# Gated recurrent stage: the next head's value projection moves from the second-direction unit to the first-direction unit

## The chip, the core and the metric

The kernel runs on one core of one Trainium2 chip. The metric is the device time of one launch in microseconds, the median over repeated runs. The engines are TensorE (PE in the profile, PEld for its weight loads), VectorE (DVE), ScalarE (ACT), GpSimd (POOL) and SyncE (SP), which issues the transfers. Each works through its own list of instructions in order and waits on semaphores that the others raise.

## The reference, cut to what matters

The program computes two transformer-like blocks on 1024 tokens of width 1024. The change touches one part of the second block, a gated linear recurrence with 4 heads of 128 channels, run forward and backward over 256 context tokens and 1024 tokens:

```
v, k_f, k_b, lf_f, lf_b = hg_in            # projections of the modulated input
q = silu(split_heads(p[..., O_Q:O_G])) * HG_DK ** -0.5
o = hgrn2_bidir(q, v, k_f, k_b, lf_f, lf_b, s0_f, s0_b)
o = o * rsqrt(mean(o * o, -1) + EPS) * hg_norm_g
hg = o * silu(p[..., O_G:O_SC])
```

For each direction a chunk of 128 tokens is computed as scores (query times key times the decay between the two tokens) times values, plus query times a state carried from chunk to chunk. Each head needs five projections of width 128: the first direction's gate logits, the values, the queries, the second direction's gate logits, and the output gate. The values of a head serve both of its directions.

## The kernel before

The stage is `stage_hgrn`. It runs eight units, (head 0, direction 0), (head 0, direction 1), (head 1, direction 0) and so on. Units 0, 2, 4 and 6 are called even here (the first direction), the others odd. Nothing is planned at build time: the order on each engine is written out by hand, and the list `jobs` gives every PSUM user one of three pairs of banks in turn, so that a job waits until the job three before it has been read.

A unit on PE, in this order: transposes of the decayed keys (L2747, "kt"), the diagonal scores (L2751), seven levels of masked scores (`level(n, l)`, eight products of 128 columns at L2729, sixteen records each), the products of keys and values (L2761, "kv"), queries times states (L2776), and last scores times values (L2787). In between stand pieces of the next unit's projections (`front`, whose products are made at L198 in `split_matmuls`): Z0 and Z1 are the gate logits, V0 and V1 the values of chunks 0 to 7 and 8 to 9, QUERY and GATE the rest. The values have tokens as rows, so V0 is 192 products of 128 columns and V1 48 of them; QUERY and GATE are 48 of 512 columns, made in two halves. An even unit projects for the odd unit after it (Z0, Z1, GATE), an odd one for the next head's even unit (Z0, Z1, V0, V1, QUERY).

A level on DVE: `subtract` makes differences of cumulated decays (L2985 and L2986, or L2989 and L2990), ACT exponentiates (L2849), `weigh` multiplies in keys and queries (L2998, L2999), PE forms the scores, and `select` merges them under a mask (L3016). There are three buffers for a level's operand, so `subtract` of level l + 2 waits for PE to have finished level l - 1. DVE also does the next unit's preparation between levels: `softplus` (L2934 to L2936), `forget` (L2945 to L2953), `key_distance` (L2963) and `decayed_keys` (L2970). The next unit's kt waits for `decayed_keys`.

The weights come through a `WeightStream` of 20 tiles of 128 columns with one raw buffer and two split ones. ACT makes the upper half of a tile (`hi`, L233) and DVE the rest (`lo`, L237). In `front` on ACT the split of tile t + 2 is placed right behind the read of the last piece that used tile t:

```
if piece in LAST and tile + 2 < 5 * HG_HEADS:
    stream.hi(act, tile + 2)
```

On DVE `weights_lo(n, piece)` runs `stream.lo` of the same tile, which waits for that `hi`. It stands in the list of DVE at fixed levels of the unit: behind level 1 for Z1, level 3 for GATE, level 5 for V1 (ahead of `key_distance`), and at the end for QUERY.

Of the kernel before, what the change touches and what calls it, by code (L numbers as in the profile page):

```python
# [26 lines left out]
P = 128  # L27
# [30 lines left out]
HG_DK, HG_HEADS, HG_WIDTH = 128, 4, 512  # L58
# [2524 lines left out]
def stage_hgrn(k):  # L2583
# [13 lines left out]
    def take(*shape):  # L2597
# [4 lines left out]
    raw_at = at[0]; take(KD, P)  # L2602
    split_at = at[0]; take(2, KD, P)
# [13 lines left out]
    NL = len(LEVELS)  # L2617
    units = [(h, d) for h in range(HG_HEADS) for d in range(2)]
# [1 line left out]


    w_src = ins["w_in_2"].rearrange("o (k p) n -> p (o k) n", p=P)
    stream = WeightStream(k, [[w_src[:, :, s * HG_WIDTH + h * P:s * HG_WIDTH + (h + 1) * P]]
                              for h in range(HG_HEADS) for s in (1, 0, 3, 2, 4)], None, raw_at, split_at, n_raw=1)


    Z0, Z1, V0, V1, QUERY, GATE = "z0", "z1", "v0", "v1", "q", "g"
    PIECES = ({Z0: 0, Z1: 0, V0: 1, V1: 1, QUERY: 2}, {Z0: 3, Z1: 3, GATE: 4})
    LAST = (Z1, V1, QUERY, GATE)

    def has(n, piece):
        return n <= last_unit and piece in PIECES[units[n][1]]

    def tile_of(n, piece):
        return 5 * units[n][0] + PIECES[units[n][1]][piece]


    jobs = [(0, "front", piece) for piece in PIECES[0]]
    for n, (h, d) in enumerate(units):
        def front_of_next(*pieces):  # L2640
            return [(n + 1, "front", piece) for piece in pieces if has(n + 1, piece)]
        jobs += [(n, "kt", 0), (n, "kt", 1)] + front_of_next(Z0) + [(n, "level", NL), (n, "level", 0)] + \
                ([(n, "ss", 0)] if d == 0 and h else []) + [(n, "kv", 0), (n, "kv", 1)] + front_of_next(Z1) + \
                [(n, "level", 1)] + front_of_next(V0, GATE) + [(n, "level", 2), (n, "level", 3)] + front_of_next(V1) + \
                front_of_next(QUERY) + [(n, "level", l) for l in range(4, NL)]
    jobs.append((last_unit + 1, "ss", 0))

    def slot(job):
# [39 lines left out]
    with nc.Block() as block:  # L2688
# [5 lines left out]
        @block.tensor  # L2694
        def _(pe):
            def front(n, piece, steps=(0, 1)):

                if not has(n, piece):
                    return
                job, tile = (n, "front", piece), tile_of(n, piece)  # L2700
                if 0 in steps:
                    stream.ready(pe, tile)
                    wait_free(pe, job)
                if piece in (V0, V1):
                    chunks = range(8) if piece == V0 else range(8, NCH)
                    for i, c in enumerate(chunks):
                        if (2 * i) // len(chunks) in steps:
                            last = split_matmuls(pe, [banks(job)[:, i * P:(i + 1) * P]],
                                                 lambda s, kt: k.hT[:, s, kt, c * P:(c + 1) * P],
                                                 lambda s, kt, i: stream.part(tile, s, kt), KD)  # L2710
                else:
                    first, end = {Z0: (0, T), Z1: (T, TT)}.get(piece, (CTX, TT))
                    spans = [(a, min(a + HALF, end)) for i, a in enumerate(range(first, end, HALF)) if i in steps]
                    last = split_matmuls(pe, [banks(job)[:, a - first:e - first] for a, e in spans],
                                         lambda s, kt: stream.part(tile, s, kt),
                                         lambda s, kt, i: k.hT[:, s, kt, spans[i][0]:spans[i][1]], KD)
                if 1 in steps:
                    last.then_inc(made[slot(job)[0]], 1)

            def chunk_job(job, chunks, fn):  # L2720
                wait_free(pe, job)
                for i, c in enumerate(chunks):
                    last = fn(banks(job)[:, i * P:(i + 1) * P], c)
                last.then_inc(made[slot(job)[0]], 1)

            def level(n, l):
                pe.wait_ge(x_ready, NL * n + l + 1)
                v = x[:, buffer(n, l), :]
                chunk_job((n, "level", l), range(T // P), lambda out, c: pe.matmul(  # L2729
                    out, v[:, c * P:(c + 1) * P], v[:, c * P:(c + 1) * P], start=True, stop=True))  # L2730

            def sum_of_squares(n, h):
                pe.wait_ge(sq_done, h)
                job = (n, "ss", 0)
                wait_free(pe, job)
                for half in range(2):
                    last = pe.matmul(banks(job)[:, half * HALF:(half + 1) * HALF], k.ones[:, :],
                                     root[:, half * HALF:(half + 1) * HALF], start=True, stop=True)
                last.then_inc(made[slot(job)[0]], 1)

            for piece in PIECES[0]:
                front(0, piece)
            for n, (h, d) in enumerate(units):
                halves = (range(8), range(8, NCH))
                pe.wait_ge(kh_ready, n + 1)
                for i in range(2):
                    chunk_job((n, "kt", i), halves[i], lambda out, c: pe.transpose(out, kh[:, c, :], k.ident[:, :]))  # L2747
                front(n + 1, Z0, (0,))
                pe.wait_ge(k_ready, n + 1)
                pe.wait_ge(q_scaled, h + 1)  # L2750
                chunk_job((n, "level", NL), range(T // P), lambda out, c: pe.matmul(  # L2751
                    out, keys[:, n % 2, CTX + c * P:CTX + (c + 1) * P], q[:, h % 2, c * P:(c + 1) * P],
                    start=True, stop=True))
                level(n, 0)
                front(n + 1, Z0, (1,))
                if d == 0 and h:
                    sum_of_squares(n, h)
                pe.wait_ge(kt_done, 2 * n + 2)
                pe.wait_ge(v_done, 2 * h + 2)
                for i in range(2):  # L2760
                    chunk_job((n, "kv", i), halves[i], lambda out, c: pe.matmul(  # L2761
                        out, kh_t[:, c, :], vals[:, h % 2, c, :], start=True, stop=True))
                front(n + 1, Z1)
                level(n, 1)
                front(n + 1, V0, (0,))
                front(n + 1, GATE, (0,))
                level(n, 2)
                front(n + 1, V0, (1,))
                front(n + 1, GATE, (1,))
                level(n, 3)  # L2770
                pe.wait_ge(states_ready, n + 1)
                pe.wait_ge(qh_ready, n + 1)
                if d == 0 and h:
                    pe.wait_ge(o_free, h)
                for c in range(T // P):
                    last = pe.matmul(o_ps[:, c * P:(c + 1) * P], states[:, c, :], qh[:, c * P:(c + 1) * P],  # L2776
                                     start=d == 0 and c % 4 == 0, stop=False, skip_group_check=True)
                last.then_inc(inter_made, 1)
                front(n + 1, V1)
                front(n + 1, QUERY, (0,))  # L2780
                level(n, 4)
                front(n + 1, QUERY, (1,))
                for l in range(5, NL):
                    level(n, l)
                pe.wait_ge(selected, n + 1)
                for c in range(T // P):
                    last = pe.matmul(o_ps[:, c * P:(c + 1) * P], vals[:, h % 2, CCH + c, :], att[:, c * P:(c + 1) * P],  # L2787
                                     start=False, stop=d == 1, skip_group_check=True)
                last.then_inc(o_made, 1)
            sum_of_squares(last_unit + 1, HG_HEADS)  # L2790

        @block.scalar
        def _(act):
# [94 lines left out]
            for n, (h, d) in enumerate(units):  # L2888
# [11 lines left out]
                front(n + 1, Z1)  # L2900
                softplus_parts(n + 1)
                level(n, 4)
                front(n + 1, V0)
                front(n + 1, GATE)
                forget_parts(n + 1)
                level(n, 5)
                front(n + 1, V1)
                level(n, 6)
                front(n + 1, QUERY)
                decays(n + 1)  # L2910
            squares(HG_HEADS - 1)
            inverse_root(last_unit + 1)
# [2 lines left out]
        def _(dve):  # L2915
            link = chained(dve, v_ord)

            def weights_lo(n, piece):

                if has(n, piece) and tile_of(n, piece) + 2 < 5 * HG_HEADS:  # L2920
                    stream.lo(dve, tile_of(n, piece) + 2)
# [148 lines left out]
            for n, (h, d) in enumerate(units):  # L3070
# [3 lines left out]
                for l in range(1, NL):  # L3074
# [14 lines left out]
                    if l == 4:  # L3089
                        forget(n + 1)  # L3090
                    if l == 5:
                        weights_lo(n + 1, V1)
                        key_distance(n + 1)
                        subtract(n + 1, 0)
                subtract(n + 1, 1)
# [381 lines left out]
```

## Time and profile before

| what | value |
|---|---|
| median of 3 runs (lowest, highest) | 2919.38 us (2919.1, 2920.84) |
| the profiled execution's own time, its span | 2910.27 us, 2908.6 us |
| PE busy over the span | 2573.3 us (88%) |
| DVE busy, ACT busy | 1631.6 us (56%), 954.0 us (33%) |
| prologue of the stage with head 0's projections | about 1480 to 1537 us |
| unit 0, first kt to the next unit's kt | 1537.0 to 1603.1 us |
| unit 1 | 1603.1 to 1668.1 us |
| units 2 and 3 | to 1732.2 and 1798.8 us |
| units 4 and 5 | to 1865.6 and 1932.2 us |
| units 6 and 7 | to 1999.2 and about 2033 us |

The busy time of PE counts matmuls at whichever clock was granted, so a slow product adds to it. A unit's length is read from the start of its kt to the start of the next. A timeline row gives start, length, engine, line, operation, output and input, count, and in brackets the idle time ahead of it and the engine and line that ended it; rows that follow one another on one engine and line are merged, and the length is that of the merged row.

### The profile page before, as it was taken

Reading aid. Unit: us, or ns where it says so; the run is one execution under the profiler, and the core shown is the slowest. Engines: PE = TensorE matmul, PEld = TensorE weight load, DVE = VectorE, ACT = ScalarE, POOL = GpSimd, SP = SyncE. Lnnn points to the kernel's source line nnn. Section 1 sums busy time; section 2 is a strip of 40 time slices with the busy share of each in tenths; the row PEclk is TensorE's granted clock in tenths of the full one; section 3 lists DMA queues with packets and bytes.
Section 4 is the critical chain, followed back from the end, with each engine's and each line's share of the span. In section 5 each row is a group of like instructions: output and inputs, shape, how many; then the busy total and the mean of one; then the engine's idle time right before and its main releaser. Section 6 shows DMA issues by size and latency. Waiting matters only on the chain. (4 is left out here: it accounts for less than half of the span.)

```text
span 2908.6 us, 39503 instructions
## 1 busy us (share of the span) xinstructions
PE 2573.3 (88%) x16801; PEld 1379.2 (47%) x16801; DVE 1631.6 (56%) x2102; ACT 954.0 (33%) x1099; POOL 34.6 (1%) x61
## 2 busy tenths in 40 slices
PE   7977685999999999998866878796887999999997
PEld 4446462444444444444434757576332444444443
DVE  6667746654444443533226666667656676766243
ACT  5115206432323231322034444554333222222221
POOL 0020000010000000000000000000000000000000
PEclk9989897999999999999778999998999999999998
DMA  9036363211121223330010000000210212122433
GB/s 305 22 102 198 108 192 116 73 41 46 43 58 43 58 80 100 100 112 19 1 44 15 23 15 23 15 16 1 73 30 15 58 43 58 43 58 80 114 100 98
DMA packets 299447, 198.99 MB, mean 68 GB/s; under 512 B 11280, under 2 KB 294062, under 8 KB 298799
## 3 DMA queue, kind: packets, MB, share of 16 engines
q1 hardware_dynamic: 298438, 196.70, 22.8%
q8 instruction: 105, 1.72, 0.3%
q10 hardware_dynamic: 873, 0.32, 0.0%
q14 instruction: 31, 0.25, 0.0%
HBM read 187.02 MB, written 9.45 MB: 68 GB/s over the span
## 5 line engine op out<-in xcount | busy, mean ns | idle before, releaser
L198 PE MATMUL ps<-hT,arena 128*128 128x512 bf16 (+1 forms) x6384 | 1388.8, 380 | 72.7 <-DVE hT L697 17.6
L198 PEld LDWEIGHTS ps<-hT,arena 128*128 128x128 bf16 x6384 | 626.7, 99 | 823.4 <-issue 45.9
L1883 PE MATMUL ps<-arena 128*128 128x512 bf16 x2112 | 458.0, 379 | 2.5 <-DVE arena L1865 2.5
L1883 PEld LDWEIGHTS ps<-arena 128*128 128x128 bf16 x2112 | 206.3, 98 | 252.0 <-DVE arena L1865 4.4
L2137 DVE SCALAR_TENSOR_TENSOR arena<-ps,vec,arena 128x945 f32<-128x945 f32 (+2 forms) x176 | 215.1, 1222 | 75.4 <-ACT arena L2123 56.0
L2104 DVE SCALAR_TENSOR_TENSOR arena<-ps,vec,arena 128x1023 f32<-128x1023 f32 (+1 forms) x88 | 106.7, 1275 | 181.0 <-ACT arena L2094 181.0
L1865 DVE TENSOR_TENSOR arena<-hT,arena 128x2816 bf16<-128x2816 f32 (+2 forms) x44 | 93.7, 2157 | 155.6 <-ACT arena L1859 155.5
L2729 PE MATMUL ps<-arena 128*128 128x128 f32 x896 | 124.2, 299 | 55.4 <-DVE arena L2999 46.3
L1859 ACT ACTIVATE arena<-hT 128x2816 bf16<-128x2816 f32 (+2 forms) x44 | 77.8, 1798 | 251.9 <-DMA hT<-w_down_dram 124.1
L2729 PEld LDWEIGHTS ps<-arena 128*128 128x128 f32 x896 | 118.1, 212 | 62.2 <-DVE arena L2999 49.1
L2050 DVE TENSOR_TENSOR arena<-hT,arena 128x2048 bf16<-128x2048 f32 x44 | 100.9, 2293 | 35.6 <-ACT arena L2016 35.6
L2094 ACT ACTIVATE arena<-ps,vec 128x1024 f32<-128x1024 f32 x44 | 50.6, 1200 | 177.6 <-PE ps L198 177.6
L2798 ACT ACTIVATE arena<-ps 128x1024 f32<-128x1024 f32 (+1 forms) x48 | 36.3, 756 | 220.6 <-PE ps L198 186.4
L2146 ACT ACTIVATE arena<-arena 128x1024 f32<-128x1024 f32 x22 | 23.2, 1057 | 230.2 <-DVEq L2141 230.2
L2016 ACT ACTIVATE arena<-hT 128x2048 bf16<-128x2048 f32 x44 | 83.4, 1895 | 16.4 <-DMA hT<-ffn_up_dram 8.2
L2063 DVE TENSOR_TENSOR arena<-arena 128x1024 f32 (+1 forms) x44 | 53.9, 1226 | 59.9 <-ACT arena L2028 59.9
L198 PE MATMUL ps<-arena,hT 128*128 128x128 bf16 (+1 forms) x1152 | 78.3, 230 | 6.5 <-PEq L158 6.5
L198 PEld LDWEIGHTS ps<-arena,hT 128*128 128x128 bf16 x1152 | 74.2, 99 | 10.2 <-issue 7.0
L1051 PE MATMUL ps<-arena 128*128 128x512 f32 x160 | 71.7, 603 | 0.8 <-ACT arena L639 0.3
L599 ACT ACTIVATE arena<-xT 128x512 f32<-128x512 f32 x64 | 39.8, 630 | 98.3 <-DVE xT L562 54.9
L2028 ACT ACTIVATE arena<-arena 128x1024 f32 (+1 forms) x44 | 46.5, 1057 | 64.4 <-DVE arena L2116 32.4
L198 PE MATMUL ps<-hT 128*128 128x512 bf16 (+1 forms) x432 | 64.4, 308 | 2.0 <-DVE hT L699 2.0
(414 smaller groups left out, 2572.2 us busy)
## 6 DMA issues: line engine op xcount, KB each, us to landing
xT<-ada_w_dram SPq DMA_DIRECT2D x24, 1024.0 KB, 5.9
hT<-w_up_dram SPq DMA_DIRECT2D x44, 512.0 KB, 5.0
hT<-ffn_up_dram SPq DMA_DIRECT2D x44, 512.0 KB, 5.0
hT<-w_down_dram SPq DMA_DIRECT2D x30, 704.0 KB, 6.6
hT<-ffn_down_dram SPq DMA_DIRECT2D x30, 704.0 KB, 7.0
arena<-w_in_dram SPq DMA_DIRECT2D x35, 512.0 KB, 4.4
xT<-w_mod_dram SPq DMA_DIRECT2D x16, 1024.0 KB, 5.6
arena<-w_mod_dram SPq DMA_DIRECT2D x8, 1024.0 KB, 19.7
```

Source lines behind the costliest of these rows:

```text
L198: last = pe.matmul(out, lhs(a, kt), rhs(b, kt, i), start=start and kt == 0 and (a, b) == (0, 0), stop=stop and kt == n_k - 1 and (a, b) == ...
L1051: last = pe.matmul(k.ps[:, 2 * p + half, :], exact[n][:, kt, :], h[:, kt, half * HALF:(half + 1) * HALF], start=kt == 0, stop=kt == KD - 1)
L1859: last = act.activation(parts[0], raw, ACT.Copy)
L1865: last = dve.tensor_tensor(parts[1], raw, parts[0], ALU.subtract)
L1883: last = pe.matmul(self.bank(u), self.part(u, a, kt), self.g[:, b, kt, cols], start=kt == 0 and (a, b) == (0, 0), stop=kt == FT - 1 and (a ...
L2016: act.activation(self.w[:, b, :, 0], self.raw, ACT.Copy).then_inc(self.hi[b], 1)
L2050: dve.tensor_tensor(self.w[:, b, :, 1], self.raw, self.w[:, b, :, 0], ALU.subtract).then_inc(self.lo[b], 1)
L2063: dve.tensor_tensor(self.g[:, 1, 2 * i + b, :], c[0], self.g[:, 0, 2 * i + b, :], ALU.subtract).then_inc(self.done[b], 1)
L2094: last = eng.activation(c[s], p[s], ACT.Identity, bias=bias[:, s, bass.ds(j, 1)], scale=w[:, 2, s, bass.ds(j, 1)])
L2104: last = eng.scalar_tensor_tensor(c[s][:, lag:T], p[s][:, 0:T - lag], w[:, tap, s, bass.ds(j, 1)], c[s][:, lag:T], ALU.mult, ALU.add)
L2137: eng.scalar_tensor_tensor(to, src[:, r0 + di:r1 + di, c0 + dj:c1 + dj], w[:, 3 * (di + 1) + dj + 1, bass.ds(j, 1)], to, ALU.mult, ALU.add ...
L2729: chunk_job((n, "level", l), range(T // P), lambda out, c: pe.matmul(out, v[:, c * P:(c + 1) * P], v[:, c * P:(c + 1) * P], start=True, st ...
```

## The change

The value projection of the next head moves one unit forward. V0 of unit n + 2 is issued on PE behind level 4 of even unit n, V1 behind level 5. They leave the odd unit, where V0 stood in halves ahead of levels 2 and 3, and V1 behind the states. The order of the weight tiles follows (values, then gate logits, then queries of the next head behind the output gate of this one). ACT reads V0 between levels 5 and 6 and V1 behind level 6, each in the even unit, and the split of the tile that comes two after the values goes with it. On DVE the matching `lo` keeps its place behind level 5, in the even unit now.

```diff
-    stream = WeightStream(k, [[w_src[:, :, s * HG_WIDTH + h * P:s * HG_WIDTH + (h + 1) * P]]
-                              for h in range(HG_HEADS) for s in (1, 0, 3, 2, 4)], None, raw_at, split_at, n_raw=1)
+    Z_OF, V_OF, Q_OF, Z2_OF, G_OF = 1, 0, 3, 2, 4
+    tiles = [(0, Z_OF), (0, V_OF), (0, Q_OF)]
+    for h in range(HG_HEADS):
+        tiles += [(h, Z2_OF), (h, G_OF)] + ([(h + 1, V_OF), (h + 1, Z_OF), (h + 1, Q_OF)] if h + 1 < HG_HEADS else [])
...
-                [(n, "level", 1)] + front_of_next(V0, GATE) + [(n, "level", 2), (n, "level", 3)] + front_of_next(V1) + \
-                front_of_next(QUERY) + [(n, "level", l) for l in range(4, NL)]
+                [(n, "level", 1)] + front_of_next(GATE) + [(n, "level", 2), (n, "level", 3)] + \
+                front_of_next(QUERY) + [(n, "level", 4)] + values_of_next(V0) + [(n, "level", 5)] + values_of_next(V1) + \
+                [(n, "level", l) for l in range(6, NL)]
...   PE
                 level(n, 1)
-                front(n + 1, V0, (0,))
                 front(n + 1, GATE, (0,))
                 level(n, 2)
-                front(n + 1, V0, (1,))
                 front(n + 1, GATE, (1,))
...
-                front(n + 1, V1)
                 front(n + 1, QUERY, (0,))
                 level(n, 4)
                 front(n + 1, QUERY, (1,))
-                for l in range(5, NL):
+                front(n + 2, V0)
+                level(n, 5)
+                front(n + 2, V1)
+                for l in range(6, NL):
                     level(n, l)
...   ACT
                 level(n, 4)
-                front(n + 1, V0)
                 front(n + 1, GATE)
                 forget_parts(n + 1)
                 level(n, 5)
-                front(n + 1, V1)
+                front(n + 2, V0)
                 level(n, 6)
                 front(n + 1, QUERY)
+                front(n + 2, V1)
                 decays(n + 1)
...   DVE
                     if l == 5:
-                        weights_lo(n + 1, V1)
+                        weights_lo(n + 2, V1)
                         key_distance(n + 1)
                         subtract(n + 1, 0)
```

## Rows read from the trace of the kernel before

**Rows 1.** Engine sums of unit 1: stretch, length, busy time (count) by engine, clock, DMA.

```profile
core 0: us, PE busy (x) PEld busy (x) DVE busy (x) ACT busy (x) POOL busy (x), PEclk, DMA share, GB/s
1603.10:1668.10 65.00, 58.75 (x552) 46.69 (x551) 45.01 (x69) 32.68 (x32) 0.00 (x0) 1.00 0.09 25
```

**Rows 2.** Timeline of PE, end of unit 0: levels 4, 5, 6, scores times values.

```profile
1580.81 2.05 PE L2729 MATMUL ps<-arena 128*128 128x128 f32 x16 [1.18 <-DVE arena L2999]
1591.64 3.78 PE L2729 MATMUL ps<-arena 128*128 128x128 f32 x16 [8.78 <-DVE arena L2999]
1596.05 3.74 PE L2729 MATMUL ps<-arena 128*128 128x128 f32 x16 [0.62 <-DVE arena L2999]
1601.23 2.05 PE L2787 MATMUL ps<-arena 128*128 128x128 f32 x16 [1.44 <-DVEq L3101]
```

**Rows 3.** Timeline of DVE, unit 0: a lo, select 4, key_distance, weigh 6.

```profile
1578.32 1.23 DVE L237 TENSOR_TENSOR arena<-arena 128x1024 bf16<-128x1024 f32 x1 [4.38 <-ACT arena L233]
...
1591.50 0.70 DVE L3016 COPY_PREDICATED arena<-masks,ps 128x512 f32<-128x512 uint32 x1
1592.10 1.49 DVE L2963 TENSOR_TENSOR arena<-arena 128x1280 f32<-128x1280 f32 x1
...
1594.70 0.69 DVE L2998 TENSOR_TENSOR arena<-arena 128x512 f32<-128x512 f32 x1
```

**Rows 4.** Timeline, unit 1: from a projection's read to the next tile's lo.

```profile
1624.63 0.38 ACT L2798 ACTIVATE arena<-ps 128x256 f32<-128x256 f32 x1 [4.33 <-PE ps L198]
1624.91 1.05 ACT L233 ACTIVATE arena<-arena 128x1024 bf16<-128x1024 f32 x1
...
1625.99 1.23 DVE L237 TENSOR_TENSOR arena<-arena 128x1024 bf16<-128x1024 f32 x1 [0.38 <-ACT arena L233]
1627.13 0.68 DVE L2998 TENSOR_TENSOR arena<-arena 128x512 f32<-128x512 f32 x1
```

**Rows 5.** Timeline, rest of unit 1 (PE, and DVE where it gates PE).

```profile
1627.77 5.52 PE L198 MATMUL ps<-arena,hT 128*128 128x128 bf16 x96
1631.04 1.49 DVE L2934 SCALAR_TENSOR_TENSOR arena<-arena 128x1280 f32<-128x1280 f32 x1 [0.76 <-ACT arena L2832]
1633.13 2.00 PE L2729 MATMUL ps<-arena 128*128 128x128 f32 x16
1634.71 0.68 DVE L2998 TENSOR_TENSOR arena<-arena 128x512 f32<-128x512 f32 x1
1640.33 2.00 PE L2729 MATMUL ps<-arena 128*128 128x128 f32 x16
1643.59 0.70 DVE L3016 COPY_PREDICATED arena<-masks,ps 128x512 f32<-128x512 uint32 x1
1643.96 2.84 PE L198 MATMUL ps<-arena,hT 128*128 128x128 bf16 x48
1646.64 5.34 PE L198 MATMUL ps<-hT,arena 128*128 128x512 bf16 x24
1651.82 1.95 PE L2729 MATMUL ps<-arena 128*128 128x128 f32 x16
1652.39 0.67 DVE L2998 TENSOR_TENSOR arena<-arena 128x512 f32<-128x512 f32 x1
1658.78 3.73 PE L2729 MATMUL ps<-arena 128*128 128x128 f32 x32
1668.13 1.25 PE L2747 MATMUL ps<-ident,arena 128*128 128x128 f32 x10
```

**Rows 6.** Engine sums of one slice at the end of unit 3, for the clock.

```profile
1794.00:1795.00 1.00, 0.00 (x0) 0.00 (x0) 1.00 (x1) 1.00 (x2) 0.00 (x0) 0.59 0.00 0
```

**Rows 7.** Timeline of PE, ends of units 1, 2 and 3.

```profile
1666.24 2.05 PE L2787 MATMUL ps<-arena 128*128 128x128 f32 x16 [3.73 <-DVEq L3101]
1726.73 2.05 PE L2729 MATMUL ps<-arena 128*128 128x128 f32 x16 [0.66 <-DVE arena L2999]
1795.28 3.78 PE L2787 MATMUL ps<-arena 128*128 128x128 f32 x16 [3.73 <-DVEq L3101]
1798.85 2.31 PE L2747 MATMUL ps<-ident,arena 128*128 128x128 f32 x10
```

More of the change, by code:

```diff
@@ L2622, in stage_hgrn @@
     w_src = ins["w_in_2"].rearrange("o (k p) n -> p (o k) n", p=P)
-    stream = WeightStream(k, [[w_src[:, :, s * HG_WIDTH + h * P:s * HG_WIDTH + (h + 1) * P]]
-                              for h in range(HG_HEADS) for s in (1, 0, 3, 2, 4)], None, raw_at, split_at, n_raw=1)
+    Z_OF, V_OF, Q_OF, Z2_OF, G_OF = 1, 0, 3, 2, 4
+    tiles = [(0, Z_OF), (0, V_OF), (0, Q_OF)]
+    for h in range(HG_HEADS):
+        tiles += [(h, Z2_OF), (h, G_OF)] + ([(h + 1, V_OF), (h + 1, Z_OF), (h + 1, Q_OF)] if h + 1 < HG_HEADS else [])
+    stream = WeightStream(k, [[w_src[:, :, s * HG_WIDTH + h * P:s * HG_WIDTH + (h + 1) * P]] for h, s in tiles],
+                          None, raw_at, split_at, n_raw=1)
     Z0, Z1, V0, V1, QUERY, GATE = "z0", "z1", "v0", "v1", "q", "g"
-    PIECES = ({Z0: 0, Z1: 0, V0: 1, V1: 1, QUERY: 2}, {Z0: 3, Z1: 3, GATE: 4})
+    PIECES = ({Z0: Z_OF, Z1: Z_OF, V0: V_OF, V1: V_OF, QUERY: Q_OF}, {Z0: Z2_OF, Z1: Z2_OF, GATE: G_OF})
     LAST = (Z1, V1, QUERY, GATE)
@@ L2634, in tile_of @@
     def tile_of(n, piece):
-        return 5 * units[n][0] + PIECES[units[n][1]][piece]
+        return tiles.index((units[n][0], PIECES[units[n][1]][piece]))
     jobs = [(0, "front", piece) for piece in PIECES[0]]
@@ L2641, in front_of_next, with values_of_next @@
             return [(n + 1, "front", piece) for piece in pieces if has(n + 1, piece)]
+        def values_of_next(piece):
+            return [(n + 2, "front", piece)] if has(n + 2, piece) else []
         jobs += [(n, "kt", 0), (n, "kt", 1)] + front_of_next(Z0) + [(n, "level", NL), (n, "level", 0)] + \
                 ([(n, "ss", 0)] if d == 0 and h else []) + [(n, "kv", 0), (n, "kv", 1)] + front_of_next(Z1) + \
-                [(n, "level", 1)] + front_of_next(V0, GATE) + [(n, "level", 2), (n, "level", 3)] + front_of_next(V1) + \
-                front_of_next(QUERY) + [(n, "level", l) for l in range(4, NL)]
+                [(n, "level", 1)] + front_of_next(GATE) + [(n, "level", 2), (n, "level", 3)] + \
+                front_of_next(QUERY) + [(n, "level", 4)] + values_of_next(V0) + [(n, "level", 5)] + values_of_next(V1) + \
+                [(n, "level", l) for l in range(6, NL)]
     jobs.append((last_unit + 1, "ss", 0))
```

## The prediction, made before the changed kernel was built or run

> **What bounds the stage now.** I read the engine sums unit by unit first, then the timeline of one even and one odd unit, engine by engine, for what ends each wait, and last the granted clock in slices of 1 us. In unit 1, an odd one, PE is busy 58.75 of 65.00 us [rows 1], and levels 2 to 6 follow on projections without a gap: it looks bound by PE. In unit 0 PE stands idle 8.78 us between levels 4 and 5 and then waits for DVE before level 6 too [rows 2], while DVE works through the next unit's preparation, select of level 4, key_distance and weigh of level 6 back to back [rows 3]. So the end of an even unit is bound by DVE, and PE has room there. The change puts 240 products into that room. The question is what else they take with them.
>
> **PE in the even unit.** V0's rate is read from the odd unit: 96 products from 1627.77 to 1633.13, 5.36 us [rows 5], so V0 takes 2 x 5.36 = 10.7 us and V1 2.68 us (1643.96 to 1646.64 [rows 5]). Behind level 4 (1580.81 [rows 2] plus 1.87 for a level, half of the 3.73 of two [rows 5], 1582.7) V0 runs to 1593.4. Level 5, ready at 1591.64 [rows 2], starts 1.8 us later, and V1 follows at 1595.2, its last product out at 1595.2 + 2.84 = 1598.1. On PE alone this is nearly free: level 6 came at 1596.05 [rows 2] and could come at 1598.
>
> **DVE in the even unit: the wait that comes with it.** The split of the tile two after the values is tied to V1: ACT does `hi` behind V1's read, and DVE's `lo` of it stands behind level 5, ahead of key_distance, in order. Such a wait exists already: DVE stood 4.38 us in front of a `lo` for ACT's `hi` in this unit [rows 3]. The steps from the read of a projection are: read to `hi` 0.28, `hi` to `lo` 1.08, `lo` to the next instruction 1.14 us [rows 4]. From 1598.1 this puts `hi` at 1598.4, `lo` at 1599.5 and key_distance at 1600.6, where it was at 1592.10 [rows 3]: 8.5 us later (7.4 of waiting, 1.1 of `lo` itself). Queued behind it on DVE are subtract of the next unit, weigh of level 6 (1594.70, so 1603.2), the last selects and decayed_keys; PE's level 6, scores times values and the next kt wait for those, ACT's key exponentials for key_distance. None has slack, so the next unit starts 8.5 us later. Least cost: nothing, if `hi` did not wait for V1 (a rival, below). V0's read by ACT at 1593.6 and the exponential of level 6 behind it, by 1596, are hidden by that wait; without it they would still be ahead of weigh of level 6. Bank turns: V0 takes the pair that select of level 2 has left, V1 that of level 4, read at 1592.2; neither waits. The transfer of that tile starts when the `lo` before it is done (1579.5) and has 19 us, so it is hidden.
>
> **The odd unit.** V0's halves stood ahead of levels 2 and 3, V1 ahead of QUERY. Not all of the 13.4 us comes back. Level 2 is then free at once, but level 3 needs weigh of level 3, at 1634.71, which stands behind softplus, and that began at 1631.04 when ACT's logarithm was done [rows 5]; neither depends on V0. A level starts 1.35 us after its weigh (1594.70 to 1596.05 [rows 2, 3]), so level 3 moves from 1640.33 to 1636.06, 4.27 us. V1 gives 2.68 more. From there PE's chain QUERY, level 4, QUERY, level 5 is solid to 1658.78, and 9.35 us of DVE work lead to kt at 1668.13 [rows 5], all unchanged: 6.95 us at full clock. DVE keeps up: select of level 3 to weigh of level 5 is at most 8.80 us [rows 5], so weigh of level 5 comes 2.5 us or more earlier, a `lo` of 1.14 behind it is gone, and level 6 followed level 5 with no gap before.
>
> **The clock.** Level 2 follows its weigh (1627.13 [rows 4]) by 1.35 and takes 2.0, so PE now stands idle from 1630.5 to 1636.06, 5.6 us. After an idle of 3.73 us the granted clock was low in unit 3 (0.59 on average in the slice before [rows 6], and scores times values took 3.78 in place of 2.05 us) and not in unit 1 [rows 7]. After 8.78 us it was low in unit 0 [rows 2]. At 5.6 us I take it as low (1.2 GHz, not 2.4). Coming back cost 1.7 on the first group and 1.1 on the transposes in unit 3 [rows 7], 2.8 us in all. It costs 0 if the clock holds, at most 3.8 if it stays low as long as in unit 0 (two levels at 3.7 in place of 1.9). I take 2.8, the row with continuous work, so the odd unit gives 6.95 - 2.8 = 4.2 us. In the even unit level 6 waits from 1598.1 to 1604.6, 6.5 us, so it is low again: in unit 0 it was anyway (3.74), in unit 2 not (2.05 [rows 7]), 1.7 us more there. Scores times values then come 5 us after the clock's return can begin; they were at full clock in unit 0, 9.6 us after level 5 began [rows 2], and low in unit 3. Between 0 and 2.8 us each, I take the middle, 1.4.
>
> **The sum.** Three even units (0, 2, 4) cost 3 x 8.5 = 25.5, the clock at level 6 in unit 2 1.7, and 3 x 1.4 = 4.2 behind it; three odd units (1, 3, 5) return 3 x 4.2 = 12.6. Units 6 and 7 have no next head. Net 18.8 us slower. The profiled execution had 2910.27 us, 9.1 under the median, and would have 2929.1; on the median of 2919.38 it is 2938.2 us.
>
> **A rule against a row.** In the trace a value product of 128 columns costs 5.36 / 96 = 56 ns from start to start [rows 5]. The Trainium skill, "TensorE: Matmul & The Clock Gate", section "Back-to-back issue gap", gives about 81 ns for a sustained stream of weight load and matmul at 128 columns. By that figure V0 and V1 would take 19.4 us, an estimate from that page, the stall would be 6.0 us longer in each even unit, and the sum 18 us higher. The trace has the same instructions, so its number stands.
>
> **Rivals.** (a) Odd units bound by PE throughout: 58.75 of 65 us busy [rows 1] speaks for it. Then all 13.4 us return, 3 x (8.5 - 13.4) = -14.7, 2904.7 us, faster. It decides where an odd unit returns more than an even one loses, 8.5 us. Against it: weigh of level 3 at 1634.71, which no products of V0 hold up, caps the first part at 4.27. 4 in 100. (b) The stall in the even unit does not come, because the split is not tied to V1 in time: then only `lo`'s 1.1 us is added, the odd units give 4.2, 3 x (1.1 - 4.2) = -9.3, 2910 us. The order in `front` on ACT speaks against it. 4 in 100. (c) The stall is there, but the clock stays up where I have it low: odd units return 6.95, even ones lose 8.5 and no more, 25.5 - 20.9 = +4.6, 2924 us; if level 6 in units 0 and 4 is also at full clock, 1.7 less twice, +1.2. V0 fills a gap that was idle, which speaks for it; the 5.6 and 6.5 us of new idle time, longer than the 3.73 after which it fell, against. 10 in 100. (d) The clock is low at every such place and scores times values too: 3 x 1.4 more and 2.8 at the end of unit 1, where it held, +25.8, 2945 us. 20 in 100, near the forecast in kind. The forecast has 62.
>
> **Numbers.** Changes under 0.2%, 5.8 us, can't be told from none. Faster: (a) and (b), 0.08. Same: (c) for the most part, 0.1. Slower: 0.82. The range reaches to (c)'s 2924 and past (d): 2924 to 2947.
>
> **What would show it.** In even units DVE idle some 7 us ahead of L237 behind level 5, released by ACT L233; key_distance (L2963) near 8.5 us later after the unit's start; PE idle 6 to 7 us ahead of level 6, V0 with no gap behind level 4. In odd units level 3 about 4.3 us earlier and PE idle 5 to 6 us ahead of it, at 3.7 us for the group when the clock was low. Unit 0 near 75 us for 66.1, unit 1 near 61 for 65.0. It is wrong if DVE has no such wait, or if unit 1 is below 57 us, or if the clock reads 1.0 at level 3.

## The result

The changed kernel takes 2929.21 us (median of 10 runs, 2923.81 to 2932.0), the kernel before 2917.14 us (median of 10 runs on the same occasions, 2910.39 to 2920.84). The ratio is 1.0042, 95% interval 1.0031 to 1.0053: slower by 12 us, clear of the noise. The forecast was 18.8 us slower, 2938.2 us, with a range from 2924 to 2947.

The profiled execution had 2929.68 us (span 2927.9), 19.4 us more than the one of before. Not all of that is the change, and that it lies so near the forecast's 18.8 is chance: the first kt of unit 0 starts at 1541.97 us for 1536.89, and nothing ahead of it differs between the kernels. Over all executions profiled here that start lay between 1535.1 and 1542.9. So the two are compared unit by unit, from kt to kt, with lengths from the starts of L2755 (L2747 before) on PE:

| unit | before | changed | difference |
|---|---|---|---|
| 0 (even) | 66.22 | 76.98 | +10.76 |
| 1 (odd) | 65.02 | 61.69 | -3.33 |
| 2 (even) | 64.09 | 74.48 | +10.39 |
| 3 (odd) | 66.63 | 61.96 | -4.67 |
| 4 (even) | 66.76 | 74.49 | +7.73 |
| 5 (odd) | 66.64 | 62.02 | -4.62 |
| 6 | 66.99 | 64.61 | -2.38 |
| 0 to 6 | 462.35 | 476.23 | +13.88 |

**The end of unit 0 after.** The timeline of PE first (start, length, engine, line, output and input, count, idle before and what ended it). Level 4, V0, level 5, V1, level 6, scores times values, the next kt answer to [rows 2]; line numbers of the changed kernel are 8 higher here.

```profile
1586.17 2.05 PE L2737 MATMUL ps<-arena 128*128 128x128 f32 x16 [1.18 <-DVE arena L3007]
1588.05 10.88 PE L198 MATMUL ps<-arena,hT 128*128 128x128 bf16 x192
1598.77 2.00 PE L2737 MATMUL ps<-arena 128*128 128x128 f32 x16
1600.61 2.84 PE L198 MATMUL ps<-arena,hT 128*128 128x128 bf16 x48
1610.18 3.78 PE L2737 MATMUL ps<-arena 128*128 128x128 f32 x16 [6.72 <-DVE arena L3007]
1615.39 3.72 PE L2795 MATMUL ps<-arena 128*128 128x128 f32 x16 [1.44 <-DVEq L3109]
1618.95 1.26 PE L2755 MATMUL ps<-ident,arena 128*128 128x128 f32 x10
```

The timeline of ACT and DVE in the same place: V1's read, `hi`, `lo`, key_distance, and weigh of level 6, which answer to [rows 3, 4].

```profile
1603.49 0.38 ACT L2806 ACTIVATE arena<-ps 128x256 f32<-128x256 f32 x1 [2.31 <-PE ps L198]
1604.00 1.06 ACT L233 ACTIVATE arena<-arena 128x1024 bf16<-128x1024 f32 x1
1605.09 1.23 DVE L237 TENSOR_TENSOR arena<-arena 128x1024 bf16<-128x1024 f32 x1 [7.54 <-ACT arena L233]
1606.23 1.48 DVE L2971 TENSOR_TENSOR arena<-arena 128x1280 f32<-128x1280 f32 x1
...
1608.84 0.68 DVE L3006 TENSOR_TENSOR arena<-arena 128x512 f32<-128x512 f32 x1
```

V0 and V1 sit in the gap in which PE was idle, and level 5 starts without a wait. But DVE stands 7.54 us in front of `lo`, until ACT has read V1 and split the tile. Everything behind it is late, and PE's idle time has moved ahead of level 6: 6.72 us, with the clock low behind it (3.78 us for a level).

Over the stage, DVE's waits for ACT's `hi` ahead of `lo`: total, times, longest. It was 12.0 us in 7 times before.

```profile
DVE arena L237 <- ACT arena L233: 34.6, 10, 7.5
```

**Unit 1 after.** The timeline of PE from level 1 to the next kt (levels 1, 2, 3, states, QUERY's first half, level 4, its second half, levels 5 and 6, scores times values, kt), answering to [rows 5, 7]:

```profile
1642.03 2.02 PE L2737 MATMUL ps<-arena 128*128 128x128 f32 x16 [1.60 <-DVEq L3057]
1644.55 2.05 PE L2737 MATMUL ps<-arena 128*128 128x128 f32 x16 [0.50 <-DVE arena L3007]
1651.88 3.78 PE L2737 MATMUL ps<-arena 128*128 128x128 f32 x16 [5.28 <-DVE arena L3007]
1655.46 2.43 PE L2782 MATMUL ps<-arena 128*128 128x128 f32 x16
1657.94 5.13 PE L198 MATMUL ps<-hT,arena 128*128 128x512 bf16 x23
1662.91 1.95 PE L2737 MATMUL ps<-arena 128*128 128x128 f32 x16
1664.69 5.34 PE L198 MATMUL ps<-hT,arena 128*128 128x512 bf16 x23
1669.87 3.73 PE L2737 MATMUL ps<-arena 128*128 128x128 f32 x32
1677.33 3.48 PE L2795 MATMUL ps<-arena 128*128 128x128 f32 x16 [3.72 <-DVEq L3109]
1680.64 1.25 PE L2755 MATMUL ps<-ident,arena 128*128 128x128 f32 x10
```

Level 2 starts at once, level 3 does not: PE waits 5.28 us for DVE's weigh. (A group of 23 products is 24 with one record missing.) The engine sums of the unit and of two slices (length, busy by engine, granted clock) answer to [rows 1, 6]. PE has lost 9.6 us of busy time and the unit 3.3 us. The clock is 1.0 at first in the idle time and 0.50, the lower of its two levels, before level 3 begins.

```profile
1618.95:1680.64 61.69, 49.17 (x308) 36.95 (x311) 43.45 (x67) 30.32 (x29) 0.00 (x0) 0.92 0.06 18
1648.00:1649.00 1.00, 0.00 (x0) 0.00 (x0) 0.97 (x2) 0.99 (x2) 0.00 (x0) 1.00 0.00 0
1650.00:1651.00 1.00, 0.00 (x0) 0.00 (x0) 1.00 (x2) 0.34 (x1) 0.00 (x0) 0.50 0.00 0
```

### The profile page after: what moved, and what is told of

The parts are those of the page before. It is cut to its first block and busy times, and to the rows that moved or that the text cites. A ratio compares the mean times of both kernels' runs of the same rounds, so it can differ in the third digit from the quotient of the medians.

```text
span 2927.9 us, 39311 instructions
## 1 busy us (share of the span) xinstructions
PE 2571.0 (88%) x16609; PEld 1386.5 (47%) x16801; DVE 1630.7 (56%) x2102; ACT 954.8 (33%) x1099; POOL 34.5 (1%) x61
## 5 line engine op out<-in xcount | busy, mean ns | idle before, releaser
L198 PEld LDWEIGHTS ps<-arena,hT 128*128 128x128 bf16 x1152 | 74.2, 99 | 10.6 <-issue 7.0
L237 DVE TENSOR_TENSOR arena<-arena 128x1024 bf16<-128x1024 f32 (+1 forms) x24 | 27.1, 1134 | 91.2 <-ACT arena L233 91.2
```

What stands on the lines that cost most here:

```text
L198: last = pe.matmul(out, lhs(a, kt), rhs(b, kt, i), start=start and kt == 0 and (a, b) == (0, 0), stop=stop and kt == n_k - 1 and (a, b) == ...
```

## The experiments

The first four ran together, the last two together, each against the kernel before on the same chip. Unit lengths are from one profiled execution each, ratios from the timed runs. Where an edit moves a PSUM user, the list `jobs` follows it, which the cuts below leave out, as they do the ACT side of experiment 3 and, in experiment 5, the move of `lo`.

| kernel | ratio to the kernel before (95%) | units 0 / 1 / 2 / 3 / 4 / 5 / 6, us |
|---|---|---|
| before | 1 | 66.22 / 65.02 / 64.09 / 66.63 / 66.76 / 66.64 / 66.99 |
| changed | 1.0042 (1.0031 to 1.0053) | 76.98 / 61.69 / 74.48 / 61.96 / 74.49 / 62.02 / 64.61 |
| 1 lo late | 0.9953 (0.9940 to 0.9967) | 66.40 / 61.56 / 65.83 / 61.35 / 66.90 / 61.82 / 64.62 |
| 2 V1 early | 1.0025 (1.0015 to 1.0035) | 73.21 / 61.84 / 74.34 / 62.18 / 74.34 / 62.19 / 64.62 |
| 3 no values | 0.9944 (0.9930 to 0.9957) | 66.42 / 61.74 / 64.09 / 62.08 / 64.09 / 62.17 / 64.61 |
| 4 filled | 1.0021 (1.0011 to 1.0031) | 77.02 / 59.80 / 76.85 / 59.79 / 76.77 / 58.10 / 64.63 |
| 5 QUERY early | 0.9910 (0.9893 to 0.9926) | 66.76 / 58.39 / 65.83 / 56.89 / 65.84 / 56.91 / 64.62 |
| 6 QUERY early, filled | 0.9890 (0.9873 to 0.9906) | 66.59 / 57.64 / 65.83 / 57.61 / 65.83 / 57.59 / 62.99 |

**1. The lo behind decayed_keys.** This asks whether the wait is the loss, or the products themselves.

```diff
                     if l == 5:
-                        weights_lo(n + 2, V1)
                         key_distance(n + 1)
...
                 decayed_keys(n + 1)
+                weights_lo(n + 2, V1)
```

> The changed kernel with one line moved on DVE: in even units the lo of the tile two after the values stands behind decayed_keys of the next unit, not ahead of key_distance. PE and ACT are unchanged. Theory (the 7.5 us wait on DVE for ACT's hi behind V1, and 1.1 us of lo, are the loss): the wait disappears from the even unit, key_distance stands directly behind select of level 4 and weigh of level 6 comes before V1 is done; level 6 is then bound by V1, 1.8 us later than in the kernel before. Even units 66 to 67 us (kernel before 66.2, 64.1, 66.8; changed 77.0, 74.5, 74.5), odd ones stay near 61.7 as in the changed kernel; in sum 9 to 13 us faster than the kernel before, 0.9955 to 0.997. Rival 1 (the 240 products themselves, in the wrong place on PE, delay the unit): even units stay near 74, ratio 1.004. Rival 2 (clock alone): even units lose 3 us at most against the changed kernel, ratio 1.002 or more.

Measured: 0.9953 (0.9940 to 0.9967), 2902.4 us. This is 13.2 us faster than the kernel before, just past the 9 to 13 expected. Even units are back at 66.40, 65.83 and 66.90 us; the products are in the same place as in the changed kernel. The timeline of its unit 0:

```profile
1589.76 0.70 DVE L3024 COPY_PREDICATED arena<-masks,ps 128x512 f32<-128x512 uint32 x1
1590.36 1.48 DVE L2971 TENSOR_TENSOR arena<-arena 128x1280 f32<-128x1280 f32 x1
...
1593.52 2.84 PE L198 MATMUL ps<-arena,hT 128*128 128x128 bf16 x48
...
1596.20 2.00 PE L2737 MATMUL ps<-arena 128*128 128x128 f32 x16
...
1601.16 1.22 DVE L237 TENSOR_TENSOR arena<-arena 128x1024 bf16<-128x1024 f32 x1
1601.54 1.25 PE L2755 MATMUL ps<-ident,arena 128*128 128x128 f32 x10
```

key_distance (L2971) stands right behind select, level 6 right behind V1, and the `lo` falls into time in which DVE waits for PE in the next unit anyway (it still stands idle 5.01 us ahead of the merge of the diagonal products at 1609.80). Both rivals fall. What made the changed kernel slower hung on the place of one DVE instruction, and with it moved the change is a gain. The products themselves are not quite free: from level 4 to level 6 unit 0 takes 17.13 us for 15.24 before, 1.9 more. Level 6 then ran in 2.00 us where it took 3.74 before at the low clock, which gives most of that back in units 0 and 4; in unit 2 level 6 had been at full clock before, and 1.7 us remain.

**2. V1 directly behind V0.** A dose: the wait should shorten by just what V1 comes earlier.

```diff
...   PE
                 front(n + 2, V0)
-                level(n, 5)
                 front(n + 2, V1)
-                for l in range(6, NL):
+                for l in range(5, NL):
...   ACT
                 front(n + 2, V0)
+                front(n + 2, V1)
                 level(n, 6)
                 front(n + 1, QUERY)
-                front(n + 2, V1)
```

> The changed kernel with V1 directly behind V0, ahead of level 5, on PE and ACT; the lo on DVE keeps its place ahead of key_distance. Theory (the wait lasts until V1 has been read and split): V1 ends 1.85 us earlier, so the wait falls from 7.5 to 5.7 us and each even unit is 1.8 us shorter, 5.5 us in all, near 75.2, 72.7 and 72.7 us, though level 5 starts 2.7 us later; ratio to the kernel before 1.002 to 1.003. Rival (products ahead of a level cost what they delay it): level 5 comes 2.7 us later and even units get longer, 77 and more, ratio 1.006 or more.

Measured: 1.0025 (1.0015 to 1.0035), as the theory had it; level 5 later did not lengthen the unit. The interval overlaps the changed kernel's (1.0031 to 1.0053), so the dose rests on the trace: in all three even units DVE waits 5.7 us ahead of `lo` for 7.5, and in PE's timeline the idle time ahead of level 6 is 4.88 us for 6.72, 1.8 less:

```profile
1599.85 2.00 PE L2737 MATMUL ps<-arena 128*128 128x128 f32 x16
1606.74 3.58 PE L2737 MATMUL ps<-arena 128*128 128x128 f32 x16 [4.88 <-DVE arena L3006]
1611.76 2.05 PE L2794 MATMUL ps<-arena 128*128 128x128 f32 x16 [1.44 <-DVEq L3108]
```

Unit 0 is 3.8 us shorter, units 2 and 4 by 0.1 only, where 1.8 was expected of each. In unit 0 the clock was back for scores times values (2.05 for 3.72); in units 2 and 4 it was not (3.79 and 3.78 for 2.05 in the changed kernel), which takes back the 1.8 us. The unit lengths of this one execution fit the dose only with that; the timed runs (1.0025 for 1.0042, 5 us of the 5.5 expected) fit it as it stands.

**3. No value projection in odd units.** One side alone: what do odd units return if nothing is paid elsewhere? Heads 1 to 3 use the values of head 0.

```diff
...   PE
-                if not has(n, piece):
+                if not has(n, piece) or (n and piece in (V0, V1)):
                     return
...
-                        out, kh_t[:, c, :], vals[:, h % 2, c, :], start=True, stop=True))
+                        out, kh_t[:, c, :], vals[:, 0, c, :], start=True, stop=True))
```

> The kernel before with the value projections of heads 1 to 3 left out on PE and ACT (no V0, V1 in units 1, 3 and 5, nothing in their place; all heads use the values of head 0; the weight tiles are still loaded and split). It measures what odd units can return when nothing is paid in the even ones. Theory (level 3 is held by softplus on DVE, clock low at level 3): units 1, 3, 5 near 61.7 us, 3.3 to 5 us less each, even ones as before; 11 to 15 us faster than the kernel before, ratio 0.995 to 0.996. Rival (odd units bound by PE throughout): 13.4 us less each, 51.6 to 53.2 us, 40 us in all, ratio 0.986.

Measured: 0.9944 (0.9930 to 0.9957), 16.4 us faster, a little more than the 11 to 15 expected. The odd units are 61.74, 62.08 and 62.17 us, those of the changed kernel to 0.2 us. So 13.4 us of PE work less in a unit buys 3.3 to 4.5 us; the rival of units bound by PE throughout falls. (The 2.7 us less in unit 4 and 2.4 in unit 6, which make up the surplus in the trace, are the clock. Before, kt took 2.31 us in unit 4 [rows 7] and 2.18 in unit 6, here 1.25; level 6 of unit 4 took 3.78 and scores times values of unit 6 3.51, here 2.05 each.) In PE's timeline level 3 waits as in the changed kernel:

```profile
1633.47 2.05 PE L2729 MATMUL ps<-arena 128*128 128x128 f32 x16 [0.54 <-DVE arena L3001]
1641.04 3.79 PE L2729 MATMUL ps<-arena 128*128 128x128 f32 x16 [5.52 <-DVE arena L3001]
1644.62 2.46 PE L2776 MATMUL ps<-arena 128*128 128x128 f32 x16
```

**4. The idle time of odd units filled, in the changed kernel.** This prices the clock at level 3.

```diff
                 level(n, 2)
+                if d == 1 and n < last_unit:
+                    wait_free(pe, (n, "level", 3))
+                    for _ in range(22):
+                        pe.matmul(banks((n, "level", 3))[:, 0:HALF], k.hT[:, 0, 0, 0:P], k.hT[:, 0, 0, 0:HALF],
+                                  start=True, stop=True)
                 level(n, 3)
```

> The changed kernel with 22 products of 512 columns (4.8 us at full clock) between levels 2 and 3 of units 1, 3 and 5, written to the banks of level 3 ahead of it and read by no one; PE stood idle there for 5.3 to 5.5 us. Theory (the clock fell in this idle time and cost 2.3 us: level 3 at 3.78 in place of 2.0, the states' group at 2.4 to 2.65 in place of 1.95): the clock reads 1.0 in this stretch, both groups take 2.0, units 1, 3 and 5 are 2.2 us shorter, 6.7 us less than the changed kernel, ratio to the kernel before near 1.002. Rival (the clock there costs nothing because DVE has slack behind it, forget of the next unit being later): level 3 is faster but the units keep 61.7 to 62.0 us, ratio 1.004.

Measured: 1.0021 (1.0011 to 1.0031). The filling, level 3, the states, and the end of unit 1 in PE's timeline:

```profile
1644.83 4.70 PE L2779 MATMUL ps<-hT 128*128 128x512 bf16 x21
1650.05 2.05 PE L2737 MATMUL ps<-arena 128*128 128x128 f32 x16 [0.53 <-DVE arena L3012]
1651.94 1.95 PE L2787 MATMUL ps<-arena 128*128 128x128 f32 x16
...
1673.35 3.78 PE L2800 MATMUL ps<-arena 128*128 128x128 f32 x16 [3.74 <-DVEq L3114]
1676.92 2.05 PE L2755 MATMUL ps<-ident,arena 128*128 128x128 f32 x10
```

(The filling is 22 products, of which one record is missing.) Both groups are at full clock, and units 1 and 3 are 1.9 and 2.2 us shorter: 22 useless products make the kernel faster. Unit 5 is 3.9 us shorter, since the clock also held at its end. Part comes back: units 2 and 4 begin with the clock low (kt at 2.05 and 2.00 us, 0.8 more) and end with it low (scores times values at 3.62 and 3.59 us for 2.05), and are 2.3 us longer. So in the profiled execution units 0 to 6 are 3.3 us shorter in sum, in the timed runs the kernel is 6 us shorter (1.0042 to 1.0021, two intervals that meet at 1.0031).

**5. QUERY's first half ahead of level 3.** The same gap filled with work that is needed, on top of experiment 1.

```diff
...   PE
                 level(n, 2)
                 front(n + 1, GATE, (1,))
+                front(n + 1, QUERY, (0,))
                 level(n, 3)
...
                 last.then_inc(inter_made, 1)
-                front(n + 1, QUERY, (0,))
-                level(n, 4)
                 front(n + 1, QUERY, (1,))
+                level(n, 4)
```

> The changed kernel with lo moved as in the first experiment, and the first half of QUERY ahead of level 3 in odd units (it stood behind the states), the second half behind the states. It puts 5.2 us of work that is needed anyway into the 5.3 us in which PE waited for softplus and the clock fell. Theory (what the odd unit did not return was this idle time with its clock): level 3 starts where it did, at full clock, QUERY's first half is off the chain, and the end of the unit is bound by DVE (forget, key_distance, last selects); units 1, 3 and 5 near 57 us for 61.7, ratio to the kernel before 0.990 to 0.992. Rival (DVE is the bound of the odd unit already, PE's order does not matter): odd units stay near 61, ratio 0.995.

Measured: 0.9910 (0.9893 to 0.9926), 2889.32 us, faster than both kernels and than experiment 1. Odd units take 58.39, 56.89 and 56.91 us. In PE's timeline of unit 1 level 3 now follows the projection, at full clock, and levels 5 and 6 wait for DVE:

```profile
1637.38 5.13 PE L198 MATMUL ps<-hT,arena 128*128 128x512 bf16 x23
1642.61 2.05 PE L2737 MATMUL ps<-arena 128*128 128x128 f32 x16
...
1654.96 2.05 PE L2737 MATMUL ps<-arena 128*128 128x128 f32 x16 [1.55 <-DVE arena L3007]
...
1659.37 2.05 PE L2737 MATMUL ps<-arena 128*128 128x128 f32 x16 [2.35 <-DVE arena L3007]
...
1664.70 3.54 PE L2795 MATMUL ps<-arena 128*128 128x128 f32 x16 [3.28 <-DVEq L3108]
```

**6. The end of odd units filled too, in the kernel of experiment 5.**

```diff
                     level(n, l)
+                if d == 1 and n < last_unit:
+                    wait_free(pe, (n + 1, "kt", 0))
+                    for _ in range(12):
+                        pe.matmul(banks((n + 1, "kt", 0))[:, 0:HALF], k.hT[:, 0, 0, 0:P], k.hT[:, 0, 0, 0:HALF],
+                                  start=True, stop=True)
                 pe.wait_ge(selected, n + 1)
```

> The fifth experiment's kernel with 12 products of 512 columns (2.6 us at full clock, read by no one, in the banks of the next kt) behind level 6 of units 1, 3 and 5, where PE waits some 3.3 us for the last select. It asks whether the clock lost at the ends of odd units (scores times values at 3.4 to 3.8 us in place of 2.05) can be held by filling. Theory (the idle time lets it fall): scores times values takes 2.05 us at the end of all three units; 0 to 2.7 us less per unit, as often as it was low in the fifth experiment; ratio 0 to 0.002 under the fifth. Rival (the products delay the last group or bring nothing): the same ratio or 0.001 more.

Measured: 0.9890 (0.9873 to 0.9906), which overlaps experiment 5's interval, so no gain over it is shown (medians of four runs each, 2883.69 and 2889.32 us). The filling and scores times values of unit 1:

```profile
1659.82 3.62 PE L2796 MATMUL ps<-hT 128*128 128x512 bf16 x11 [0.22 <-issue]
1663.28 1.95 PE L2800 MATMUL ps<-arena 128*128 128x128 f32 x16
```

Scores times values took 1.95 us in all three odd units. But in each of them the clock had already fallen while level 6 ran (2.47, 3.00 and 3.51 us for 2.05) and came back only within the filling or as it began (3.62, 3.08 and 2.55 us for 11 recorded products, which take some 2.5 at full clock), so the filling ended later than the wait it filled. In unit 1 the granted clock still read 1.00 in the 2.36 us in which PE stood idle ahead of level 6, which started at 1657.13, and until 1658.5 us, and 0.50 at 1659.0: it fell when PE was at work again. In two of the three units experiment 5 had this group at full clock without it and was 0.7 us shorter (56.89 and 56.91 for 57.61 and 57.59); in the first it was 0.75 longer.

## Why the prediction was right, step by step

**The wait on DVE.** Right in mechanism and close in size. DVE waited 7.54 us where 7.4 was worked out, and key_distance comes 9.05 us later after the unit's kt (64.26 for 55.21) where 8.5 was. The surplus is 0.3 in the clock at the start of unit 0, and 0.23 in one step: from V1's read to `hi` it was 0.51 us, not the 0.28 of [rows 4]. That row is Z1's, which `hi` follows directly. Behind V1's read ACT first waits until the read has landed and raises `v_done` (`signal` in `front`). V1's own rows of before, in the timeline of ACT in unit 1, have 0.48 and were the ones to take:

```profile
1649.06 0.36 ACT L2798 ACTIVATE arena<-ps 128x256 f32<-128x256 f32 x1
1649.54 1.06 ACT L233 ACTIVATE arena<-arena 128x1024 bf16<-128x1024 f32 x1
```

No run took that signal out, so that it is the reason is read from the code. Level 4 to level 6, free of the unit's start, grew by 8.77 us in unit 2 (15.24 to 24.01). Experiment 1 shows the cause: with that wait moved away, even units are within 0.2 us (0 and 4) and 1.7 us (2) of before, and experiment 2 shows the dose.

**PE in even units.** V0 took 10.72 us to the next start and V1 followed 1.84 us behind level 5, as said. That is 55.8 ns per product; the 81 ns of the Trainium skill ("TensorE: Matmul & The Clock Gate", "Back-to-back issue gap") again did not show.

**The odd unit.** 6.95 us less the clock at level 3. Measured, level 3 and the states cost 1.73 + 0.48 = 2.2 us more for the low clock, where 2.8 was taken from a row of another place; 6.95 - 2.2 = 4.75, less 1.4 in unit 1, whose last group fell to the low clock (3.48 for 2.05), is the 3.33 measured. Units 3 and 5 returned 4.67 and 4.62, more than the 4.2 forecast. The sum of the three, 12.6, is the forecast's by luck: the clock at level 3 was priced too high (2.8 for 2.2 to 2.4 us), and the clock lost at the end of unit 1 was left out of the forecast (it stood in rival (d)). Experiment 3 shows the cap by itself, and experiment 4 gives 1.9 and 2.2 us back in units 1 and 3.

**The clock at the end of even units.** Level 6 was low in all three, as taken. Scores times values fell to the low clock in one of three (3.72, 2.05 and 2.05 us): 1.7 us for the 4.2 of the sum.

**The sum.** 18.8 predicted for the stage, 13.9 measured. The terms that lower it are all of the clock: 2.5 at scores times values of even units, 1.0 in unit 4, which had begun low before and did not after, and 2.4 in unit 6, which had begun low (0.9) and ended low (1.5) before and did neither after; the forecast let them be. The 1.0 the other way is the longer wait: 8.77 us for 8.5 three times, and 0.3 at the start of unit 0. The 2.4 in unit 6 is neither a cost nor a return of that unit's own work, which is the same in both kernels. The timed runs say 12 us. The forecast lies above that by more than the noise, within its range. Rival (c), the clock up at every such place, gave 4.6 us, about as far off on the other side, but the trace rules it out: level 3 took 3.78 us in all three odd units and level 6 in all three even ones. Rival (d), the clock low everywhere, was further off. (a) is excluded by experiment 3, (b) by the wait of 7.54 us in the changed kernel's own trace.

**Not settled.** Whether the clock falls at a given end of a unit is not predicted by anything shown here. An idle time of 3.7 us kept it in unit 1 of before [rows 7] and at the end of unit 5 of experiment 4, and lost it in the changed kernel's odd units. All unit lengths are from one execution each, so terms of 1 to 2 us that hang on the clock may come out otherwise in another.

## What to carry to other kernels

When work moves into another engine's idle time, follow the bookkeeping tied to it (here the split of a later weight tile) to the engine that does it, and look at what stands behind it in that engine's list: the 13.4 us of products cost 1.9 us at most, while moving the one waiting DVE instruction took 7.6 to 10.6 us off each even unit, slow products behind it included, and turned +0.4% into -0.5%. Removing work from a busy engine returns only what lies up to the next wait on someone else: here 3.3 to 4.7 of 13.4 us. Pulling needed work into the hole that was left raised this to 6.6 to 9.7 us per unit, and the gain from 0.5% to 0.9%. An idle stretch of PE costs its own length and, where the clock falls, the slow products behind it. And when a step's price is read from a row, take the row of the same step: two reads of the same shape differed by 0.2 us, with a wait and a signal behind only one of them.

## What was not expected of the hardware

Two things. Products that no one reads, put into an idle stretch of PE, shortened the kernel by 6 us (1.0042 to 1.0021), though part of the clock kept in one place was lost at the next. And in experiment 6 the clock fell not in PE's idle time but 0.3 to 1.4 us after PE had begun level 6, so that products put right behind level 6 came too late to hold it.
